# Token-mixer tiles: index pairs two at a time, token shift ahead of the rotations, decay and gate work inside the dense tiles, output stored in parts

## The reference

```python
for l in range(2):                       # first_block
    x = x + 0.5 * swiglu(rms_norm(x, ffn_norm[l, 0]), ...)
    p = rms_norm(x, mix_norm[l]) @ w_in[l]
    pa, pb, pc = split_cols(p, GROUP_SPLITS)
    ya = dsa_attention(pa, att_q_norm[l], att_k_norm[l])
    yb, v_first = rwkv7_time_mix(pb, ...)
    yc = gated_deltanet(pc, ...)
    x = x + concat([ya, yb, yc]) @ w_out[l]
    x = x + 0.5 * swiglu(rms_norm(x, ffn_norm[l, 1]), ...)
return second_block(x, ...)
```

## Time and profile before

| what | us |
|---|---|
| median of 3 runs (lowest, highest) | 3575.18 (3574.53, 3580.99) |
| the profiled execution's own time | 3576.05 |
| its span, from the first to the last instruction | 3574.3 |
| TensorE busy | 3423.1 |
| VectorE, ScalarE, GpSimd busy | 1408.8, 1249.7, 1660.1 |
| first mixer: from tile att 4 to the end of tile rec 14 | 411.2 to 568.4 |
| first mixer: attention items | 576.2 to 644.7 |
| first mixer: recurrences, to the first tile of mix_out | 644.7 to about 806 |
| second mixer: the end of tile rec 14, item 0's first product | 1758.3, 1766.9 |

### The profile page before, as it was taken

How to read it: one execution, slowest core, us unless ns; L and a number is a source line. 1 busy time by engine, 2 the same in 40 slices (tenths; PEclk the granted TensorE clock), 3 DMA queues, 4 the chain that set the end, 5 groups by cost and what they waited for, 6 DMA issues and landing times.

```text
span 3574.3 us, 47700 instructions
## 1 busy us (share of the span) xinstructions
PE 3423.1 (96%) x17140; PEld 2813.0 (79%) x17140; DVE 1408.8 (39%) x2740; ACT 1249.7 (35%) x1881; POOL 1660.1 (46%) x2052
## 2 busy tenths in 40 slices
PE   7999998799999999999878999999899999999999
PEld 6888775688888888887658888888767888888887
DVE  4431477855321322236787442215563110341100
ACT  3222335534222422233463432223533332433321
POOL 5765542004665566644300266644403555435553
PEclk9999998899999999999889999999999999999999
DMA  4443221003443344322100144432202322213222
GB/s 176 145 141 112 83 77 50 16 1 107 148 145 118 118 147 143 125 91 77 65 25 1 57 145 146 135 101 89 77 1 71 100 94 98 73 65 101 99 94 94
DMA packets 100319, 335.25 MB, mean 94 GB/s; under 512 B 10800, under 2 KB 16592, under 8 KB 100064
## 3 DMA queue, kind: packets, MB, share of 16 engines
q1 hardware_dynamic: 83920, 277.83, 23.4%
q10 hardware_dynamic: 16272, 55.65, 4.6%
HBM read 330.78 MB, written 2.65 MB: 93 GB/s over the span
## 4 chain that ended last, share of the span: by engine, by line
issue 40%; POOL 32%; PE 27%; DVE 1%; POOLq 0%; ACT 0%; DVEq 0%
POOL w_lo L654 32%; PE ps L2159 7%; PE ps L2160 7%; PE ps L2161 7%; PE ps L2937 1%; PE ps L2916 0%; PE ps L2182 0%; PE ps L2925 0%; PE ps L2183 0%; PE ps L2187 0%; PE ps L3027 0%; DVE stat L2064 0%; DVE sq L2057 0%; PE ps L3033 0%; PE ps L2917 0%
## 5 line engine op out<-in xcount | busy, mean ns | idle before, releaser
L654 POOL TENSOR_TENSOR w_lo<-w_raw,w_hi 128x256 fp32r<-128x256 f32 x2040 | 1653.4, 843 | 1890.9 <-ACT w_hi L697 1884.3
L2159 PE MATMUL ps<-h_hi,w_hi 128*128 128x512 f32 x2624 | 1030.8, 393 | 0.9 <-ACT mem L899 0.9
L2161 PE MATMUL ps<-h_hi,w_lo 128*128 128x512 f32 x2624 | 1021.6, 389 | 0.0
L2160 PE MATMUL ps<-h_lo,w_hi 128*128 128x512 f32 x2624 | 1021.1, 389 | 0.0
L697 ACT ACTIVATE w_hi<-w_raw 128x1024 fp32r<-128x1024 f32 x510 | 538.5, 1058 | 931.5 <-DMA w_raw<-in_tiles 931.5
L2159 PEld LDWEIGHTS ps<-h_hi,w_hi 128*128 128x128 f32 x2624 | 492.6, 188 | 118.2 <-issue 14.3
L2160 PEld LDWEIGHTS ps<-h_lo,w_hi 128*128 128x128 f32 x2624 | 492.7, 188 | 104.4 <-issue 3.4
L2161 PEld LDWEIGHTS ps<-h_hi,w_lo 128*128 128x128 f32 x2624 | 492.5, 188 | 102.3
L2160 PE MATMUL ps<-a_lo,w_hi 128*128 (+1 forms) x1120 | 435.7, 389 | 0.0
L2159 PE MATMUL ps<-a_hi,w_hi 128*128 (+1 forms) x1056 | 410.8, 389 | 0.0
L2161 PE MATMUL ps<-a_hi,w_lo 128*128 (+1 forms) x1056 | 410.8, 389 | 0.0
(11 more groups left out here) (473 smaller groups left out, 3646.2 us busy)
## 6 DMA issues: line engine op xcount, KB each, us to landing
w_raw<-in_tiles SPq DMA_DIRECT2D x510, 512.0 KB, 3.3
ada_raw<-in_ada_tiles ACTq DMA_DIRECT2D x96, 512.0 KB, 3.3
x<-in_x_t SPq DMA_DIRECT2D x2, 1024.0 KB, 6.4
sq<-in_cond ACTq DMA_DIRECT2D x4, 512.0 KB, 4.0
mem<-gates SPq DMA_DIRECT2D x8, 256.0 KB, 4.0
out_t<-x SPq DMA_DIRECT2D x1, 2048.0 KB, 7.1
consts<-in_consts SPq DMA_DIRECT2D x1, 1280.0 KB, 12.6
core_mem<-gates SPq DMA_DIRECT2D x8, 128.0 KB, 2.8
```

What stands on the lines that cost most here:

```text
L654: ins = nc.gpsimd.tensor_tensor(w_lo[:, s, part], w_raw[:, s, part], w_hi[:, s, part].bitcast(F32), ALU.subtract)
L2159: nc.tensor.matmul(bank, wh, hi, start=first, stop=False, skip_group_check=True)
L2160: nc.tensor.matmul(bank, wh, lo, start=False, stop=False, skip_group_check=True)
L2161: return nc.tensor.matmul(bank, wl, hi, start=False, stop=last, skip_group_check=True)
```

## The change

Index pairs 0 to 3 stand two to a tile, at tiles 6 and 7, and pairs 4 to 11 at tiles 8 to 15, two tiles earlier than before; pairs 1 and 3 use banks 4 and 7. The rotations of the index queries move with them. VectorE derives a few masks early. The heads are spread at tiles rec 4 to 6 (before: rec 6 to 10), and four rounds of best keys go ahead of the first scaling. The token shift comes before the rotations of q and k, which TensorE starts at tiles rec 8, 10 and 11. The decay and `a` part of the lora products stands at the end of tile rec 10, the `g` part at rec 12, with the sum and the spread for the norm of `kk` at rec 12 and 13; ScalarE's activations and VectorE's cumulative sums go along. The `meanwhile` work that is left moves to earlier items. The last store is made of one DMA for half of `x` and four for one chunk each.

```diff
-        FIRST_INDEX_TILE = 6
+        INDEX_TILES = {6: (0, 1), 7: (2, 3), **{p + 4: (p,) for p in range(4, len(INDEX_PAIRS))}}
+        ROT_QI = {4: (0,), 5: (1, 2), 6: (3,)}
+        def index_banks(p):
+            return (4, 7) if p in (1, 3) else (5, 6)
+        HEADS_AT = {4: (0, 1), 5: (2, 3), 6: (4,)}
+        ROT_AT = {8: (0, 1), 10: (2, 3), 11: (4,)}
+        LORA_TILE, GATE_TILE = 10, 12
...
-            sp.dma_start(out.rearrange("(k p) t -> p k t", p=P), x[:, :, :]).then_inc(S["out_stored"], 16)
+            sp.wait_ge(S["x_ready"], updated - KD // 2)
+            sp.dma_start(out_t[:, low:high, :], x[:, low:high, :]).then_inc(S["out_stored"], 16)
+            for d, k in enumerate(last_half):
+                sp.wait_ge(S["x_ready"], updated - KD // 2 + d + 1)
+                sp.dma_start(out_t[:, k, :], x[:, k, :]).then_inc(S["out_stored"], 16)
...
# ScalarE, in the loop over the rec tiles
-                    if m == REC_TILES - 2:
+                    if m == LORA_TILE:
                         act.wait_ge(S["shifted"], l + 1)
                         nc.scalar.activation(lg[0:32, :], lg[0:32, :], ACT.Tanh)
                         nc.scalar.activation(lg[64:128, :], lg[64:128, :], ACT.Sigmoid).then_inc(S["lora_in"], 1)
+                        act.wait_ge(S["kk_in"], l + 1)
+                        nc.scalar.activation(mem[:, U_KK_SQ:U_KK_SQ + 2, :], mem[:, U_KK:U_KK + 2, :], ACT.Square)
...
                     round_tile(base + m + 4)
+                    if m == LORA_TILE:
+                        act.wait_ge(S["lora_ready"], 2 * l + 1)     # four sigmoids, then beta
+                    if m == GATE_TILE:
+                        act.wait_ge(S["lora_ready"], 2 * l + 2)     # two copies, then the roots for kk
+                    if m == GATE_TILE + 1:
+                        act.wait_ge(S["decay_in"], l + 1)           # three large exponentials
...
# behind the tiles, ahead of the items
+                act.wait_ge(S["sp_in"], l + 1)
+                link(nc.scalar.activation(soft, soft, ACT.Exp))
+                nc.scalar.activation(soft, soft, ACT.Ln, bias=eps(EPS_ONE)[ROW_A:ROW_A + 4, :]).then_inc(S["sp_ln"], 1)
...
# VectorE
+                for part, units in enumerate(((), (0, 1), (2, 3), (4,))):
+                    for s in units:
+                        scale_head(s)
+                    best_keys(1, range(4 * part, 4 * part + 4))
...
+                dve.wait_ge(S["head_done"], head0 + 5)   # behind the token shift and kk
+                rope(U_K, cos, sin)
+                rope(U_K + 1, cos, sin)
...
+                dve.wait_ge(S["gates_ready"], 2 * l + 1)  # then the sums, softplus' input, kk's norm
...
# VectorE's meanwhile: same work, other items
-                    if 16 <= i < 28:
+                    if 10 <= i < 22:
...
# TensorE, in the loop over the rec tiles
-                    if 6 <= m < 11:
-                        if m >= 8:
-                            pe.wait_ge(S["head_done"], head0 + m - 7)
-                        head_spread(mem[:, 33 + m - 6, :], 4 + m % 2).then_inc(S["head_spread"], 1)
+                    for s in HEADS_AT.get(m, ()):
+                        if s >= 2:
+                            pe.wait_ge(S["head_done"], head0 + s - 1)
+                        head_spread(mem[:, 33 + s, :], 4 + s % 2).then_inc(S["head_spread"], 1)
+                    if m == LORA_TILE:
+                        pe.wait_ge(S["lora_in"], l + 1)
+                        lora_products(((4, 0), (6, 32)), 32)
+                    if m == GATE_TILE:
+                        lora_products(((2, 64),), 64)
+                        head_sums(mem_units(U_KK_SQ, U_KK_SQ + 1), 4).then_inc(S["head_sum"], 1)
+                    if m == GATE_TILE + 1:
+                        for c in range(2):
+                            ins = head_spread(mem[:, U_KK_SQ + c, :], 4 + c)
```

More of the change, by code:

```diff
@@ L889, in index_relus @@
                     w = (n + 1) * P
-                    for x in range(2):
+                    for x, bank in enumerate(index_banks(p)):
                         i = due("relu") - 1
@@ L1533, in attention @@
                 head0 = seen.get("head_done", 0)
[L1534 to L1553, removed]
@@ new lines, in attention @@
+                due("head_done", 5)
+                dve.wait_ge(S["proj_out"], first + ATT_TILES + 7)
+                V.tensor_tensor(mem[:, 2:6, :], rw[:, 0:4, 0:T], rw[:, 0:4, 1:T + 1], ALU.subtract)
+                link(V.tensor_tensor(mem[:, 33:36, :], rw[:, 4:7, 0:T], rw[:, 4:7, 1:T + 1], ALU.subtract))
+                for c in range(7):
+                    step = mem[:, 2 + c if c < 4 else 33 + c - 4, :]
+                    ins = V.scalar_tensor_tensor(rw[:, c, 1:T + 1], step, param(f"mu{l}", c), rw[:, c, 1:T + 1], ALU.mult, ALU.add)
@@ new lines, in attention @@
+                ins.then_inc(S["shifted"], 1)
+                dve.wait_ge(S["shifted"], l + 1)
+                r, k, v = (rw[:, c:c + 2, 1:T + 1] for c in (0, 2, 4))
+                kk, bonus, conv = (core_mem[:, u:u + n, :] for u, n in ((R_KK, 2), (R_SQ, 2), (G_CONV, 6)))
+                kk_unit = mem[:, U_KK:U_KK + 2, :]
+                for c in range(2):
+                    V.tensor_scalar(kk_unit[:, c, :], k[:, c, :], param(f"k_k{l}", c), None, ALU.mult)
+                    ins = V.tensor_scalar(stat[:, ST_OMKA + c:ST_OMKA + c + 1], param(f"k_a{l}", c), -1.0, 1.0, ALU.mult, ALU.add)
@@ L1558, in attention @@
                 link(ins)
-                dve.wait_ge(S["shifted"], l + 1)
+                for s in range(2, 5):
+                    rope(U_K + s, cos, sin)
+                dve.wait_ge(S["gates_ready"], 2 * l + 1)
+                for c in range(2):
+                    for n in range(TB):
+                        ins = V.tensor_tensor_scan(mem[:, 4 + c, blk(n)], const("ones"), mem[:, c, blk(n)], 0.0, ALU.mult, ALU.add)
+                link(ins)
+                cum = by_block(mem[:, 4:6, :])
@@ L1561, in attention @@
                 dve.wait_ge(S["w_used"], BASE[f"rec_in{l}"] + REC_TILES)
[L1562 to L1566, removed]
@@ L2414, in attention @@
[L2414 to L2431 removed]
+                pe.wait_ge(S["gates_ready"], 2 * l + 2)
@@ L2432, in meanwhile @@
+                pe.wait_ge(S["head_done"], due("head_done"))
+                def meanwhile(i):
+                    bonus = [core_mem[:, R_SQ + c, :] for c in range(2)]
                     rows = slice(ROW_A, ROW_A + 4)
-                    if i == 9 and l > 0:
-                        pe.wait_ge(S["head_done"], seen["head_done"] + 1)
+                    if i == 1 and l > 0:
+                        pe.wait_ge(S["proj_out"], seen["proj_out"])
                         for c in range(2):
@@ L2437, in meanwhile @@
                         ins.then_inc(S["vd_ready"], 1)
-                    if i == 12 and l > 0:
+                    if i == 4 and l > 0:
                         pe.wait_ge(S["vd_out"], 1)
```

231 lines of the change are left out of this document (110 added, 121 removed).

## The result

| | before | after |
|---|---|---|
| median, us | 3577.25 (5 runs) | 3597.88 (5 runs, 3596.30 to 3599.36) |
| ratio, 95% interval | | 1.0057 (1.0045 to 1.0068) |
| profiled execution, own time / span | 3576.05 / 3574.3 | 3597.88 / 3596.1 |

A forecast was written before the change was run, and what follows sets the result against it. TensorE was taken to bound the dense tiles, VectorE and a chain of engines the items. Per mixer 8.0 + 4.9 + 2.5 + 2.8 − 15.2 + 1.0 = +4.0, twice, less 4.1 for the store: 3579 us, range 3558 to 3592.

The forecast's parts named there:

- Term 1: Dense tiles: lora products, sums and spreads moved there add 8.0 us a mixer; index pairs, rotations and head spreads add nothing.
- Term 2: End of rec 5: TensorE stalls for VectorE's first scaling, +4.9 us a mixer (0 to 7).
- Term 3: Behind the rec 5 stall: TensorE's clock falls to half, +2.5 us a mixer (0 to 2.9).
- second rival: Tiles behind rec 10: clock falls at the second stall too and stays low, 0.4 + 2.9 more a mixer, 3586; chance 0.12.
- Term 4: Rec 10: TensorE waits for the lora input from ScalarE's tanh and sigmoid, +2.8 us a mixer (0 to 5).
- Term 5: Items to item 24: the stretch shortens as VectorE's work leaves, −15.2 us a mixer (−9 to −18).
- third rival: Items: ScalarE bounds them, VectorE idle 6 instead of 2.7 and 3.5 owed at item 24, 3591; chance 0.13.
- Term 6: Behind item 24: ScalarE pays owed work before the recurrences, +1.0 us a mixer (0 to 3.5); the recurrences are untouched.
- Term 7: End of the run: only 256 KB leave after the last x, −4.1 us, once (−3.8 to −4.3).
- The rule on table switches: ScalarE's tanh, sigmoid and softplus: a switch costs about 2.66 us, 5.5 more a mixer, 3590; chance 0.05.

The follow-up runs named there:

- e2: The changed kernel with VectorE's first scalings put back ahead of the four rounds on 256 elements; 3587.45 us, ratio 1.0024.
- e4: The changed kernel with the edits of e1 and e3 together; 3583.64 us, ratio 1.0016.
- e8: The kernel of e7 with VectorE taking the bonus product behind item 11 instead of item 9; 3567.92 us, ratio 0.9975.
- e1: The changed kernel with head groups 2 and 3 spread at rec 6 and group 4 at rec 7, a tile later; 3581.60 us, ratio 1.0010.
- e10: The kernel of e8 with VectorE's product of key unit and decay behind items 0 and 1 instead of ahead of them; 3570.19 us, ratio 0.9979.
- e3: The changed kernel with the decay and a part of the lora products at rec 11 instead of rec 10; 3585.76 us, ratio 1.0015.
- e5: The kernel before the change with only the last store in five parts; 3571.47 us, ratio 0.9985.
- e6: The kernel of e4 with VectorE's rotations of the keys put back ahead of the token shift; 3572.44 us, ratio 0.9984.
- e7: The kernel of e6 with softplus' exponential and logarithm on ScalarE behind the copy of rec 13, not the last tile; 3569.42 us, ratio 0.9977.
- e9: The kernel of e6 with the head groups back at rec 4, 5 and 6; 3586.73 us, ratio 1.0027.
- e11: The kernel of e8 with two of ScalarE's three large exponentials moved behind item 1's exponential; 3562.54 us (4 runs), ratio 0.9956.

## Why the prediction was wrong

- **Term 1, work put into the tiles, +8.0.** Right in size: 7.3. That is what remains of the 22.0 in the first mixer without the waits (5.8, 3.1 and the small one of 0.9) and the slow clock (1.5 behind rec 5, 3.4 behind rec 10). "At nothing" for the index pairs and the spreads left out that small wait.
- **Term 2, the wait at rec 5, +4.9.** Right in place, cause and queue, 0.9 to 1.2 too small. e2 moved it by 4.0, the 3.9 that the prediction gave the four rounds.
- **Term 3, the clock, +2.5.** This is the step that failed in the tiles. The drop behind rec 5 costs only 1.5, but there is a second behind rec 10, of 3.4, and in the second mixer one of 1.7 behind the small wait: 4.9 and 6.7 us of slow clock where the sum had 2.5. The prediction had the second drop as its second rival, at 0.12, and priced it at 3.3 a mixer; it was the case. Having taken one stall's drop as likely, I had no reason to take the other's as unlikely.
- **Term 4, the wait at rec 10, +2.8.** Right (3.1).
- **Term 5, the items, −15.2.** The step that failed here is its "2.7 of idle time that stays". The first 7.4, to the logarithm, were 7.2 (590.5 to 597.7), and VectorE's work from there on was the 38.5 of the sum. But up to 641.65 it is idle 5.5 us, 3.3 of them for the bonus sum alone, so 2.6 less are won. The idle times of before were measured with VectorE as the late one; with 12 us of work taken from its queue and 5.5 brought forward, it waits more for the others. This reason is argued from the rows, and no run tests it alone. The third rival had idle time of 6, but by ScalarE and with 3.5 owed at item 24. Here TensorE released 4.0 of it and ScalarE 1.2, and 0.7 was owed.
- **Term 6, "these are untouched".** Wrong for the recurrences: +2.8 and +2.3, by a lower clock on the same work, which had no term.
- **Term 7, the store, −4.1.** Mis-sized by 1.0: a part of 256 KB landed in 2.0 us, under the 3.3 of 512 KB by more than I took.
- **The rule on table switches** was rightly set aside: from the load at 552.89 the sigmoid starts at 554.19, 1.3 later, with no further piece between. By the Trainium skill (ScalarE: Activation LUTs, What ACT_TABLE_LOAD costs) it would have been about 2.66.

Over both mixers the sum misses 18.9: tiles 9.6, items 4.8, recurrences 5.1, last items −0.6. Of the tiles' 9.6, slow clock makes 6.6 and waits 4.5, and the work was 1.5 less. So TensorE's clock makes 11.7 of the 18.9: it is the largest thing that the prediction had wrong. No term had the wrong sign. But several of the unknown costs lay together on their dear side, while the range was built as if one rival at a time could be true; the combination of the second and third rival, 3597, was in none of the cases. That it equals the measured time would have been partly luck, since the recurrences' 5.1 and the waits' 4.5 stand in neither.

What stays open is what starts the long slow stretch in the recurrences. By the profiles it came in the first mixer of after, e2, e4 and e8 and in the second of after, e1, e2 and e10, with waits in the tiles and without; in neither mixer of before, e3, e5, e6, e7, e9 and e11. No run here separates its cause. Nor does one separate why the clock fell without a wait in e6.

## What to carry to other kernels

Work that is moved from a stretch with slack into one where an engine is 99.7% busy costs its whole length there, so it must take more than that from the other stretch; here 7.3 us a mixer bought 12.6, and the stalls and the clock ate the rest. Even with the stalls mended (e6) small waits and slow clock in the tiles and the recurrences ate it. When a wait is taken away, look for the next thing in the same queue before counting the gain: single edits gave 16 and 12, both together 14, and only with VectorE's order changed as well came the rest. Cases that can be true together should be priced together.

## What the runs showed of the hardware

TensorE's clock can stay at its lower level (0.50, 1.2 GHz) through work without a gap: in the first mixer of after from 692.7 to 719, where the same instructions before regained 1.00 some 4 us after they began. It can also fall with no gap just ahead of it, as in e6 behind the small products of rec 12. The long slow stretch may be what splits the runs of one kernel into groups; e3's ten lie at 3581.0 to 3581.5 and at 3585.5 to 3588.8, with a mean clock of 0.977 to 0.978 in the first and 0.974 to 0.976 in the second. Only one execution of each was profiled, so this isn't shown.

A VectorE operation's time also depends on its company: the seven steps of the token shift took 7.97, 7.62 and 6.54 us in after, before and e1, with GpSimd busy for 7.9, 6.9 and 4.0 us beside them. Steps with GpSimd at work beside them took up to 1.23, and the last three in e1, of which these windows show the start, 0.74 each (fifth busy time: GpSimd).

```profile
537.50:542.00 4.50, 4.50 (x22) 3.72 (x21) 4.50 (x5) 0.60 (x1) 4.00 (x4) 1.00 0.23 71
542.00:544.00 2.00, 2.00 (x11) 1.65 (x10) 2.00 (x4) 0.78 (x1) 0.00 (x0) 1.00 0.27 102
```
